# Two hybrid layers on one core: the convolution branch moved to the end, the sample states among the retention gates

## Chip, core and metric

The kernel runs on one core of a Trainium2 chip. The metric is the device time of one execution in microseconds: the median of 3 runs. TensorE (PE in the profile) multiplies, VectorE (DVE) and ScalarE (ACT) work on elements, GpSimd (POOL) does too and issues most of the small DMAs here, SyncE (SP) issues the weight loads.

## What is computed

Two layers on 256 prompt tokens and 8 sample tokens together, T = 264 columns, model width 1024. A layer (shortened from the reference):

```python
u = rmsnorm(h, norm_g);  z = u @ w_in
s5_out   = s5_branch(z[S5], h0, ...)        # complex diagonal state space, 32 groups x 64 states
ret_out  = retention_branch(z[Q], z[K], z[V], z[G], S0)   # 4 heads, key 128, value 256
conv_out = conv_branch(z[CONV], buf, ...)   # GLU, depthwise width 31, layer norm, silu
gates = sigmoid(z[GATE])
merged = gates[0] * (s5_out @ s5_proj) + gates[1] * (ret_out @ ret_proj) + gates[2] * (conv_out @ conv_proj)
h = h + merged @ w_out
h = h + (swiglu(rmsnorm(h)) if layer == 0 else moe_swiglu(rmsnorm(h)))   # top 2 of 8 experts

# state space:   h_t = lbar * h_(t-1) + Bbar u_t,   y = Re(C h) + D u, gelu, GLU
# retention:     inner = (q k^T * decay) v,   out = inner + (q S) * cross_decay
#                S' = gamma^c S + (k * k_decay)^T v;  group norm over the 256 values, times silu(g)
```

For a sample token the retention state of each head (128 x 256) is loaded, multiplied by gamma, gets the outer product of k and v, gives q S, and is stored: 8 samples x 4 heads, 512 KB a sample. The prompt starts from zero states. All arithmetic is fp32; the large products are made of three fp32r products of split operands.

## The kernel before, in words

Every engine has one program, written out by hand, and semaphores between them. Activations lie as [feature, token], so a tile of output is [128, 264], one PSUM bank. `tile_order()` lists all tiles in the order in which TensorE makes them; a tile's number modulo 8 is its bank, and a bank is opened when whoever evicts it has counted it. The same list orders the weights: `weight_tile` (L583) walks over blocks of 128x128, eight a chunk, in a ring of five chunks that SP fills. ScalarE makes the high part of each chunk (L976), VectorE the low part (L1283), both up to two chunks ahead of the tile that they are evicting. Three products of 264 columns a block (L577 to L579) give the tile. So where a helper of VectorE waits for something, the weights' low parts behind it wait too.

In a layer the order on TensorE is: convolution gate and value (cb, ca), state space input (zs), q, k, v; transposes (vt, vs, kt, ks: v and k as [token, feature], for prompt and samples), the state space matrices (win, kk), which GpSimd prepares; per head scores, output, state (sc, ou, st: L700 to L719), with one head's scores computed ahead; the state space drive of each 8-token chunk (si, L732); the convolution's layer norm sums (cm, cv, by ones, L610); then the sample loop, for b in 0..7: convolution gate gc(b) (8 blocks), the sample output os(b-1) (q times state, L749), convolution projection pc(b) (4 blocks), the outer products oa(b), ob(b) (L763); then the group norm sums (gm, gv, L610), the state space output y, the swish gates gg, yt, retention gate and projection gr, pr, the GLU gl, state space gate and projection gs, ps, the output wo, and the feed-forward part. Layer 0's is dense, layer 1's runs over experts.

VectorE does the 124 depthwise taps (31 by 4 blocks, L1377) in pieces: 16 beside zs, 32 beside v, 44 behind kt, 8 after each head's decay multiply (L1303). Then the 8 samples' convolution (L1303, L1460, L1462), the mean (L1468), the reciprocal (L1483). In the sample loop it steps the state space recurrence over 32 chunks of 8 tokens, 4 steps a sample, 5 small operations a step (tile rec), updates the sample's state (L1507) and masks k so that one row is left (L1475). ScalarE evicts, makes squares, roots (L1016), silus and high parts (L990).

GpSimd prepares the state space matrices (powers by doubling, L1746 to L1761), then issues: convolution states out (L1865, L1866), retention prompt state out (L1869), and per sample the store (L1873) and, when it has landed, the load of the sample after next (L1878) into one of two buffers. It prepares layer 1 after pr(7) of layer 0.

## Time and profile before

| | us |
|---|---|
| median of 3 runs | 2074.55 (2072.83 to 2078.42) |
| the profiled execution | 2078.8 |
| its span | 2076.7 |
| PE busy | 1953.4 (94%) |
| DVE busy | 1585.2 (76%) |
| ACT busy | 1171.4 (56%) |
| POOL busy | 348.5 (17%) |
| layer 1's experts, 1077 to 2067 | 990 |

Times in the rows are microseconds from the start of the span. "Busy" of PE is modelled for pipelined products. A stage's price is the stretch between two of its neighbours' starts on PE, and what stands in brackets behind a timeline row is how long the engine had been idle before it and who released it. A wait for several semaphores is put down to the last.

### The profile page before, as it was taken

What the parts mean: (1) busy time and instruction counts of PE and PEld (TensorE: products, weight loads), DVE (VectorE), ACT (ScalarE), POOL (GpSimd) and SP (SyncE); (2) the same over time, 40 slices, a digit from 0 to 9 for tenths busy, and PEclk for the clock granted to TensorE, in tenths of its full rate; (3) what the DMA queues carried; (4) which work ended last, traced back from release to release, by engine and by line L of the source; (5) the groups of instructions that cost most, each with busy time, mean ns of one, the idle gap of its engine ahead of it and who ended that gap; (6) DMA issues with size and microseconds to landing.
All of it is one profiled execution on the core that took longest, in us unless ns stands there. A gap on an engine that the chain in (4) does not pass through costs nothing.

```text
span 2076.7 us, 32156 instructions
## 1 busy us (share of the span) xinstructions
PE 1953.4 (94%) x12016; PEld 1657.9 (80%) x12016; DVE 1585.2 (76%) x1980; ACT 1171.4 (56%) x1209; POOL 348.5 (17%) x423
## 2 busy tenths in 40 slices
PE   7777999979998978999989999999999999999995
PEld 7766889979998977889977777777777777777774
DVE  6998855766545996746558888888888888888886
ACT  5333245444444443254456777767767776777775
POOL 7982100993000130100000000000000000000000
PEclk9989999989999997999969999999999999999998
DMA  5438625535555746535639999999999999999996
GB/s 195 143 91 137 219 75 167 184 110 183 183 173 154 213 101 137 157 112 181 242 141 355 368 383 351 387 360 365 371 370 378 354 379 364 370 371 366 382 358 233
DMA packets 98102, 527.57 MB, mean 254 GB/s; under 512 B 11864, under 2 KB 13432, under 8 KB 54360
## 3 DMA queue, kind: packets, MB, share of 16 engines
q1 hardware_dynamic: 86167, 488.69, 64.4%
q0 software_dynamic: 10784, 36.50, 8.2%
q8 instruction: 65, 1.06, 0.2%
q10 hardware_dynamic: 1056, 1.08, 0.1%
q14 instruction: 30, 0.24, 0.0%
HBM read 505.69 MB, written 20.54 MB: 253 GB/s over the span
## 4 chain that ended last, share of the span: by engine, by line
PE 78%; DVE 9%; POOL 6%; issue 3%; ACT 3%; DMA 1%; DVEq 0%; ACTq 0%; SPq 0%; POOLq 0%
PE bank L577 23%; PE bank L579 23%; PE bank L578 23%; POOL s5m L1761 3%; DVE zone L1377 3%; PE bank L763 1%; PE bank L749 1%; POOL work L1761 1%; DVE s5m_parts L1678 1%; PE bank L610 1%; PE bank L917 1%; PE bank L792 1%; PE bank L788 1%; ACT zone_parts L1229 1%; PE bank L872 1%
## 5 line engine op out<-in xcount | busy, mean ns | idle before, releaser
L1678 DVE TENSOR_TENSOR s5m_parts<-s5m,ring_parts 128x2048 fp32r<-128x2048 f32 x228 | 519.3, 2288 | 77.3 <-ACT ring_parts L1229 77.1
L1283 DVE TENSOR_TENSOR ring_parts<-ring,ring_parts 128x1024 fp32r<-128x1024 f32 x238 | 311.5, 1310 | 223.2 <-ACT ring_parts L976 221.9
L1229 ACT ACTIVATE ring_parts<-s5m 128x2048 fp32r<-128x2048 f32 x228 | 431.6, 1915 | 87.8 <-DMA s5m<-in_experts 81.7
L577 PE MATMUL bank<-uT_parts,ring_parts 128*128 128x264 f32 x1312 | 386.2, 294 | 39.4 <-DVE uT_parts L1300 21.0
L578 PE MATMUL bank<-uT_hi,ring_parts 128*128 128x264 f32 x1312 | 379.5, 289 | 0.0
L579 PE MATMUL bank<-uT_hi,ring_parts 128*128 128x264 f32 x1312 | 378.6, 289 | 0.0
L577 PE MATMUL bank<-s5m_parts,work_parts 128*112 128x512 f32 x896 | 359.1, 401 | 0.3 <-DVE table_parts L1671 0.3
L976 ACT ACTIVATE ring_parts<-ring 128x1024 fp32r<-128x1024 f32 x238 | 251.3, 1056 | 190.5 <-PE bank L579 169.0
L1678 DVE TENSOR_TENSOR s5m_parts<-s5m,zone_parts 128x2048 fp32r<-128x2048 f32 x112 | 255.9, 2288 | 67.1 <-ACT zone_parts L1229 66.9
L577 PEld LDWEIGHTS bank<-uT_parts,ring_parts 128*128 128x128 f32 x1312 | 254.4, 194 | 51.8 <-issue 45.5
L578 PEld LDWEIGHTS bank<-uT_hi,ring_parts 128*128 128x128 f32 x1312 | 255.3, 195 | 0.1
L579 PE MATMUL bank<-ring_parts,work_parts 128*112 128x512 f32 x640 | 254.1, 397 | 0.0
L579 PEld LDWEIGHTS bank<-uT_hi,ring_parts 128*128 128x128 f32 x1312 | 253.8, 193 | 0.0
L578 PE MATMUL bank<-ring_parts,table_parts 128*112 128x512 f32 x640 | 253.1, 396 | 0.0
L1229 ACT ACTIVATE zone_parts<-s5m 128x2048 fp32r<-128x2048 f32 x112 | 213.0, 1915 | 36.9 <-DMA s5m<-in_experts 35.3
L577 PEld LDWEIGHTS bank<-s5m_parts,work_parts 128*112 128x112 f32 x896 | 156.7, 175 | 49.5 <-issue 0.4
L577 PE MATMUL bank<-zone_parts,ring_parts 128*128 128x264 f32 x592 | 174.7, 295 | 8.8 <-DVE zone_parts L1300 8.8
L577 PE MATMUL bank<-s5m_parts,zone_parts 128*112 128x512 f32 x448 | 177.1, 395 | 0.0
L578 PEld LDWEIGHTS bank<-ring_parts,table_parts 128*112 128x112 f32 x640 | 113.0, 176 | 36.0
L579 PEld LDWEIGHTS bank<-ring_parts,work_parts 128*112 128x112 f32 x640 | 112.0, 175 | 37.1
L577 PEld LDWEIGHTS bank<-zone_parts,ring_parts 128*128 128x128 f32 x592 | 112.9, 191 | 10.4 <-issue 7.8
L1377 DVE SCALAR_TENSOR_TENSOR zone<-zone,vecs 128x256 f32<-128x256 f32 x240 | 117.1, 557 | 0.0
(283 smaller groups left out, 3126.5 us busy)
## 6 DMA issues: line engine op xcount, KB each, us to landing
s5m<-in_experts SPq DMA_DIRECT2D x340, 1024.0 KB, 6.7
ring<-in_weights SPq DMA_DIRECT2D x238, 512.0 KB, 3.3
work<-in_sret POOLq DMA_DIRECT2D x16, 512.0 KB, 4.7
out_ret_s<-work POOLq DMA_DIRECT2D x16, 512.0 KB, 4.8
s5m<-kscr POOLq DMA_DIRECT2D x16, 256.0 KB, 10.9
xT<-in_xT SPq DMA_DIRECT2D x1, 1056.0 KB, 5.1
zscr<-zone ACTq DMA_DIRECT2D x2, 528.0 KB, 5.8
work<-in_bc POOLq DMA_DIRECT2D x2, 512.0 KB, 4.9
```

The source lines that it names most:

```text
L577: pe.matmul(out, left[0], right[1], start=first, stop=False)
L578: pe.matmul(out, left[1], right[0], start=False, stop=False)
L579: return pe.matmul(out, left[0], right[0], start=False, stop=last)
L610: mm = pe.matmul(out[:, 0:T], ones[:, :], terms(i), start=(i == 0), stop=(i == n - 1))
L749: mm = pe.matmul(out[:, x:x + 1], sring[:, b % 2, h, half * P:(half + 1) * P], qs[:, h, b:b + 1], start=True, stop=True)
L763: mm = pe.matmul(out[:, x * DV:(x + 1) * DV], kmask[0:NS, b % 2, h * P:(h + 1) * P], vst[0:NS, h * DV:(h + 1) * DV], start=True, stop=True)
L976: act.activation(weights_hi(c), weights(c, ring), ACT.Copy).then_inc(high_done, 1)
L1229: act.activation(high_slot(c), slot(c, s5m), ACT.Copy).then_inc(high_done, 1)
L1283: dve.tensor_tensor(weights(c, ring_parts), weights(c, ring), f32(weights_hi(c)), ALU.subtract).then_inc(low_done, 1)
L1377: dve.scalar_tensor_tensor(out=cT[:, m, 0:SEQ], in0=xc[:, m, k:k + SEQ], scalar=vec(l, V_DWW, m * TAPS + k), in1=cT[:, m, 0:SEQ], op0=ALU. ...
L1678: dve.tensor_tensor(slot(c, s5m_parts), slot(c, s5m), f32(high_slot(c)), ALU.subtract).then_inc(low_done, 1)
L1761: last = pool.tensor_tensor(out[:, js], x[:, js], y[:, js], op)
```

## The change

It changes six things in each layer.

- The score product of the next head is no longer computed ahead: sc, ou, st for each head.
- The convolution's norm, gates and projections (cm, cv, gc, pc) move behind the state space projection: cm after ps(3), cv after ps(5), gc and pc after ps(7), before wo. The taps spread over more stages, by `CONV_AT` (how many a call, for layer 0 and layer 1). In layer 0, 0 beside zs, 8 beside v, 28 behind kt, 16 in the heads, 8 behind si, 48 beside pr, 16 in gs; in layer 1, 12, 24, 28, 12, 6, 32, 10.
- The sample loop stands beside the swish gates gg (8 blocks, no projection). The outer products take fp32r operands stacked on 72 rows (high, low, high part of v; high, high, low of k). The sample output is a product of q masked to one row, [128 x 8] by [128 x 256] for each head, all samples summed into one bank, copied and transposed once (ot). Banks: 7 rotate, the eighth takes long tiles. gr(0) stands before ot, gr(1) after y.
- The state space recurrence of 32 steps becomes a sweep. GpSimd makes the powers of the phase of lambda^8 (`turns`, by doubling, 5 complex products) and a damping tile; VectorE turns the drive back by them, scans it with real damping (two `tensor_tensor_scan` of 512 elements), and turns it forward again, at samples 2 to 6 of the loop.
- Four buffers for the sample states in place of two; sample b+4 is loaded into sample b's buffer.
- GpSimd issues the loads of samples 2 and 3 behind the convolution state's stores, makes the turns after si(3), and only then goes on to the stores. ScalarE masks k in VectorE's place. The preparation of layer 1 begins after the GLU.

```diff
+ROTATING = 7
+STACK = 72
+CONV_AT = {"zs": (0, 3), "v": (1, 3), "kt": (28, 28), "ret": (4, 3), "si": (8, 6), "gr": (6, 4), "gs": (6, 4)}
...
-        o += [((l, "sc", 0), 0)]
         for h in range(HEADS):
-            if h + 1 < HEADS:
-                o += [((l, "sc", h + 1), 0)]
-            o += [((l, "ou", h), 0), ((l, "st", h), 0)]
-        add("si", 4); add("cm", 1); add("cv", 1)
...
+            o += [((l, "sc", h), 0), ((l, "ou", h), 0), ((l, "st", h), 0)]
+        add("si", 4)
+        for b in range(NS):
+            o += [((l, "gg", b), KD)]
+            if b > 0:
+                o += [((l, "os", b - 1), 0)]
+            o += [((l, "oa", b), 0), ((l, "ob", b), 0)]
+        o += [((l, "os", NS - 1), 0), ((l, "gr", 0), KD), ((l, "ot", 0), 0)]
...
             o += [((l, "gs", d), KD), ((l, "ps", d), 4)]
+            if d == 3:
+                add("cm", 1)
+            if d == 5:
+                add("cv", 1)
+        for d in range(KD):
+            o += [((l, "gc", d), KD), ((l, "pc", d), 4)]
...
                     pe.wait_ge(*out_of((l, "ob", b)))
-                    for x in range(KD):
-                        h, half = x // 2, x % 2
-                        mm = pe.matmul(out[:, x:x + 1], sring[:, b % 2, h, half * P:(half + 1) * P],
-                                       qs[:, h, b:b + 1], start=True, stop=True)
+                    for h in range(HEADS):
+                        mm = pe.matmul(out[32 * h:32 * h + NS, 0:DV], qm[:, h, b * NS:(b + 1) * NS], states[b % 4][:, h, :],
+                                       start=False, stop=(b == NS - 1))
...
-                            mm = pe.matmul(out[:, x * DV:(x + 1) * DV], kmask[0:NS, b % 2, h * P:(h + 1) * P],
-                                           vst[0:NS, h * DV:(h + 1) * DV], start=True, stop=True)
+                            mm = pe.matmul(out[:, x * DV:(x + 1) * DV], kmask_parts[0:STACK, b % 2, h * P:(h + 1) * P],
+                                           vst_parts[0:STACK, h * DV:(h + 1) * DV], start=True, stop=True)
...
+                    act.activation(kmask_parts[0:STACK, b % 2, :], f32(kst_parts[0:STACK, :]), ACT.Copy,
+                                   scale=pick[0:STACK, b:b + 1]).then_inc(kmask_ready, 1)
...
+            def sweep(l, d):
...
+                if d == 2:
+                    dve.wait_ge(turns_ready, l + 1)
...
+                    mul(driven, si[:, :, :, 0:NC], both).then_inc(dve_order, 1)
+                    mul(swept[:, 0], si[:, 1, :, 0:NC], im).then_inc(dve_order, 1)
...
+                elif d == 3:
+                    link(add(driven[:, 0], driven[:, 0], swept[:, 0]))
+                    link(dve.tensor_tensor(driven[:, 1], driven[:, 1], swept[:, 1], ALU.subtract))
+                    link(dve.tensor_tensor_scan(swept[:, 0].rearrange("p j t -> p (j t)"), damp,
+                                                driven[:, 0].rearrange("p j t -> p (j t)"), 0.0, ALU.mult, ALU.add))
...
+                for d in range(KD):
+                    merge("gs", "ps", 0, d)
+                    if d < 3:
+                        conv_ops(l, "gs")
+                    if d == 2:
...
+                        sampled_conv()
+                    if d == 4:
+                        conv_mean()
+                    if d == 5:
+                        conv_norm()
...
+                pool.wait_ge(mm_done, DONE[(l, "si", 3)])
...
+                n = 1
+                while n < NC:
+                    product([turns[:, r, :, n:2 * n] for r in range(2)], [turns[:, r, :, 0:n] for r in range(2)],
+                            [turns[:, r, :, n - 1:n].broadcast_to([P, GJ, n]) for r in range(2)], cross[:, :, 0:n])
+                    n *= 2
...
-                    if b + 2 < NS:
+                    if b + 4 < NS:
 
                         pool.wait_ge(mm_done, DONE[(l, "os", b)])
-                        pool.wait_ge(s_out[b % 2], 16 * (4 * l + b // 2 + 1))
+                        pool.wait_ge(s_out[b % 4], 16 * (2 * l + b // 4 + 1))
```

GpSimd's program of layer 0, from the matrices' way through memory to the first samples. Before:

```order
L1859 DMA s5m<-kscr 16x32x128 x8
L1865 DMA out_conv_p<-zone 512x1x30
L1866 DMA out_conv_s<-zone 4096x1x30
L1869 DMA out_ret_p<-zone 128x4x256
L1873 DMA out_ret_s<-work 128x4x256
L1878 DMA work<-in_sret 128x4x256
L1873 DMA out_ret_s<-work 128x4x256
L1878 DMA work<-in_sret 128x4x256
```

After, with the turns between the prompt state's store and the first sample's:

```order
L1995 DMA zone<-in_sret 128x4x256 x2
L1996 DMA out_ret_p<-zone 128x4x256
L2001 COPY s5m<-lw 128x16 x2
L2002 COPY s5m<-lw 128x512
L2003 MEMSET s5m 128x16
L1872 TENSOR_TENSOR s5m<-s5m 128x16 x2
L1878 TENSOR_TENSOR s5m<-s5m 128x16
L1872 TENSOR_TENSOR s5m<-s5m 128x16 x2
L1881 TENSOR_TENSOR s5m<-s5m 128x16
L1872 TENSOR_TENSOR s5m<-s5m 128x16x2 x2
L1878 TENSOR_TENSOR s5m<-s5m 128x16x2
```

Twelve more rows of such products follow (to 128x16x16) before `L2013 DMA out_ret_s<-work 128x4x256`, which came right behind the prompt state's store.

VectorE in layer 0, the samples' convolution and the layer norm. Before, ahead of the sample loop (cT lies in zone):

```order
L1303 TENSOR_TENSOR tmp<-zone,vecs 128x248
L1460 TENSOR_REDUCE zone<-tmp 128x8
L1462 TENSOR_SCALAR zone<-zone,vecs 128x8
L1303 TENSOR_TENSOR tmp<-zone,vecs 128x248
L1460 TENSOR_REDUCE zone<-tmp 128x8
L1464 TENSOR_SCALAR zone<-zone,vecs 128x8
L1468 SCALAR_TENSOR_TENSOR zone<-bank,zone 128x1056
L1475 TENSOR_SCALAR work<-work,ident 8x512 x2
L1483 RECIPROCAL rstd<-bank 128x264
L1303 TENSOR_TENSOR zone<-zone,rstd 128x1056
L1300 TENSOR_TENSOR zone_parts<-zone,sq_parts 128x264 x4
```

After, it stands in the state space gates gs, between merges (tmp<-bank,gate is gate times projection), with the weights' low parts:

```order
L1344 TENSOR_TENSOR ring_parts<-ring,ring_parts 128x1024 x2
L1364 TENSOR_TENSOR tmp<-bank,gate 128x264
L1367 TENSOR_TENSOR zone<-zone,tmp 128x264
L1640 SCALAR_TENSOR_TENSOR zone<-bank,zone 128x1056
L1344 TENSOR_TENSOR ring_parts<-ring,ring_parts 128x1024
L1364 TENSOR_TENSOR tmp<-bank,gate 128x264
L1367 TENSOR_TENSOR zone<-zone,tmp 128x264
L1647 RECIPROCAL rstd<-bank 128x264
L1364 TENSOR_TENSOR zone<-zone,rstd 128x1056
L1344 TENSOR_TENSOR ring_parts<-ring,ring_parts 128x1024 x2
L1364 TENSOR_TENSOR tmp<-bank,gate 128x264
L1367 TENSOR_TENSOR zone<-zone,tmp 128x264
```

The same two operations of the norm (the mean, now L1640, and the reciprocal, now L1647) have five low parts and three merges between and behind them.

VectorE in the sample loop of layer 0, one sample. Before, with its four recurrence steps (tile rec):

```order
L1283 TENSOR_TENSOR ring_parts<-ring,ring_parts 128x1024 x2
L1303 TENSOR_TENSOR zone<-bank,gate 128x264
L1507 SCALAR_TENSOR_TENSOR work<-work,bank 128x256 x4
L1475 TENSOR_SCALAR work<-work,ident 8x512
L1303 TENSOR_TENSOR rec<-s5m,l 128x32
L1303 TENSOR_TENSOR rec<-s5m,l 128x16 x2
L1306 TENSOR_TENSOR rec<-rec,work 128x32
L1306 TENSOR_TENSOR s5m<-rec 128x32
L1303 TENSOR_TENSOR rec<-s5m,l 128x32
```

After, samples 2 and 3 with the sweep's first pieces:

```order
L1344 TENSOR_TENSOR ring_parts<-ring,ring_parts 128x1024
L1586 SCALAR_TENSOR_TENSOR work<-work,bank 128x256 x4
L1364 TENSOR_TENSOR s5m<-work,s5m 128x1024
L1364 TENSOR_TENSOR s5m<-work,s5m 128x512 x2
L1344 TENSOR_TENSOR ring_parts<-ring,ring_parts 128x1024
L1586 SCALAR_TENSOR_TENSOR zone<-zone,bank 128x256 x4
L1367 TENSOR_TENSOR s5m<-s5m 128x512
L1486 TENSOR_TENSOR s5m<-s5m 128x512
L1487 SCALAR_TENSOR_TENSOR s5m<-s5m 128x512
L1344 TENSOR_TENSOR ring_parts<-ring,ring_parts 128x1024
```

The small operations are gone; a sample has a wide piece of the sweep in their place.

## Rows read from the trace of the kernel before

**Rows 1.** The chain that ended last, pieces in order of time: start us, us, what
```profile
176.74 2.06 PE bank L610 x8
...
185.34 1.82 DVE rstd L1483
...
211.79 1.92 PE bank L763 x8
...
259.75 3.56 PE bank L610 x8
...
868.05 7.56 PE bank L610 x20
```

**Rows 2.** Windows: window, us, busy us (x instructions) of PE, PEld, DVE, ACT, POOL, PEclk, DMA share, GB/s
```profile
172.00:191.00 19.00, 11.79 (x154) 10.16 (x149) 9.48 (x19) 8.60 (x14) 0.79 (x1) 0.91 1.07 98
191.00:260.00 69.00, 66.62 (x457) 60.99 (x458) 57.84 (x231) 18.85 (x32) 11.65 (x16) 0.95 0.68 208
...
1077.00:2067.00 990.00, 973.08 (x4368) 735.45 (x4367) 837.95 (x544) 713.15 (x488) 27.03 (x32) 0.99 0.96 361
```

**Rows 3.** Timeline of PE: start us, us, engine line op out<-in [idle before <-releaser]
```profile
152.09 0.70 PE L700 MATMUL bank<-zone 128*128 128x256 f32 x2
...
161.81 0.60 PE L712 MATMUL bank<-work,zone 128*128 128x256 f32 x2
...
163.99 0.59 PE L700 MATMUL bank<-zone 128*128 128x256 f32 x2
...
171.34 3.94 PE L732 MATMUL bank<-s5m 128*64 128x48 f32 x128
...
191.50 0.56 PE L577 MATMUL bank<-zone_parts,ring_parts 128*128 128x264 f32 x1 [3.78 <-DVE zone_parts L1300]
...
748.84 0.70 PE L700 MATMUL bank<-zone 128*128 128x256 f32 x2
...
756.93 1.19 PE L712 MATMUL bank<-work,zone 128*128 128x256 f32 x2 [6.52 <-DVE work L1303]
```

**Rows 4.** Timeline of ACT, 379 to 384 us
```profile
379.10 0.39 ACT L1164 ACTIVATE gate<-bank 128x264 f32<-128x264 f32 x1 [1.77 <-PE bank L579]
...
383.48 0.39 ACT L1164 ACTIVATE gate<-bank 128x264 f32<-128x264 f32 x1 [0.34 <-PE bank L579]
```

**Rows 5.** Timeline of POOL, 239 to 246 and 365 to 390 us
```profile
239.92 0.75 POOL L1873 DMA_DIRECT2D out_ret_s<-work  x1 [1.34 <-DVE work L1507]
245.44 0.76 POOL L1878 DMA_DIRECT2D work<-in_sret  x1 [4.76 <-PE bank L579]
...
365.09 0.73 POOL L1746 TENSOR_TENSOR work<-work 128x16 f32<-128x16 f32 x2
...
374.60 4.07 POOL L1807 COPY work<-work 128x32 f32<-128x32 f32 x8
...
379.71 1.31 POOL L1746 TENSOR_TENSOR work<-lw,work 128x256 f32<-128x256 f32 x2
...
386.00 3.11 POOL L1761 TENSOR_TENSOR s5m<-work 128x256 f32<-128x256 f32 x3
```

**Rows 6.** DMA issues of 160 to 230 us: KB each, median us to landing
```profile
work<-in_sret POOLq DMA_DIRECT2D x5, 512.0 KB, 4.6
...
out_ret_s<-work POOLq DMA_DIRECT2D x4, 512.0 KB, 5.1
...
out_conv_s<-zone POOLq DMA_DIRECT2D x1, 480.0 KB, 27.6
```

**Rows 7.** Groups on DVE, 205 to 253 us: out<-in xcount | busy, mean ns | idle before
```profile
L1283 DVE TENSOR_TENSOR ring_parts<-ring,ring_parts 128x1024 fp32r<-128x1024 f32 x9 | 11.0, 1226 | 1.8 <-ACT ring_parts L976 1.6
L1507 DVE SCALAR_TENSOR_TENSOR work<-work,bank 128x256 f32<-128x256 f32 x24 | 8.9, 416 | 1.4 <-PE bank L763 1.2
```

**Rows 8.** Groups on DVE, 376 to 403 us, beside POOL's preparation
```profile
L1283 DVE TENSOR_TENSOR ring_parts<-ring,ring_parts 128x1024 fp32r<-128x1024 f32 x9 | 13.7, 1520 | 4.6 <-ACT ring_parts L976 4.6
```

**Rows 9.** Timeline of DVE, the first operation of the sampled convolution
```profile
171.94 0.40 DVE L1303 TENSOR_TENSOR tmp<-zone,vecs 128x248 f32<-128x248 f32 x1
```

More of the change, by code:

```diff
@@ L135, in tile_counts @@
     place, done, chunk = {}, {}, []
-    n = b = 0
+    n = b = turn = long = 0
     for i, (key, blocks) in enumerate(tile_order()):
-        place[key] = i
+        if key[1] == "os" or i > 0 and key[1] in ("ms1", "ms2"):
+            place[key] = long * NBANK + ROTATING
+            long += key[1] != "os" or key[2] == NS - 1
+        else:
+            place[key] = turn // ROTATING * NBANK + turn % ROTATING
+            turn += 1
         if key[1] in ("ms1", "ms2") and i > 0:
@@ new lines, in _, with gate_of @@
+                masked(0)
+                masked(1)
+                for b in range(NS):
+                    key = (l, "gg", b)
+                    full(key)
+                    act.activation(mT[:, b, :], at(key)[:, 0:T], ACT.Silu).then_inc(freed(key), 1)
+                    if b + 2 < NS:
+                        masked(b + 2)
+                def gate_of(name, d, of):
+                    key = (l, name, d)
+                    full(key)
+                    act.activation(gate[:, of, :], at(key)[:, 0:T], ACT.Sigmoid).then_inc(freed(key), 1)
@@ new lines, in _ @@
+                key = (l, "os", NS - 1)
+                copy_out(key, os_rows, at(key)[:, 0:DV])
+                gate_of("gr", 0, 0)
+                key = (l, "ot", 0)
+                full(key)
+                for half in range(2):
+                    last = act.activation(vT[:, half:KD:2, SEQ:T],
+                                          at(key)[:, half * P:(half + 1) * P].rearrange("p (h x) -> p h x", h=HEADS)[:, :, 0:NS],
+                                          ACT.Copy)
+                last.then_inc(freed(key), 1)
@@ new lines, in _, with merge @@
+                for d in range(KD):
+                    key = (l, "pr", d)
+                    evicted_by_act((l, "gr", d))
+                    full(key)
+                    dve.wait_ge(gated, KD * (l + 1))
+                    mul(mT[:, d, :], at(key)[:, 0:T], gate[:, d % 2, :]).then_inc(freed(key), 1)
+                    if d == 4:
+                        for m in range(4):
+                            low((l, "y", m), yg[:, m, :])
+                    conv_ops(l, "gr")
+                def merge(gate_name, proj_name, turn, d):
+                    key = (l, proj_name, d)
+                    evicted_by_act((l, gate_name, d))
+                    full(key)
+                    mul(tmp[:, d % 2, :], at(key)[:, 0:T], gate[:, d % 2, :]).then_inc(freed(key), 1)
+                    evicted_by_act(key)
+                    if turn == 0:
+                        evicted_by_act((l, "pr", d))
+                    else:
+                        dve.wait_ge(merged, 16 * l + d + 1)
+                    add(mT[:, d, :], mT[:, d, :], tmp[:, d % 2, :]).then_inc(merged, 1)
```

452 lines of the change are left out of this document (252 added, 200 removed).

## The prediction, made before the result was known

> **What bounds the kernel now.** The profiled execution took 2078.8 us, with a span of 2076.7, against a median of 2074.55 (2072.83 to 2078.42). I sum against the execution's own time and take 4.25 off at the end.
>
> I read first the chain that ended last, for the places where it leaves TensorE, then the stretches in a table of windows, then TensorE's, ScalarE's and GpSimd's timelines there. The expert half, 990 us of layer 1, has TensorE at 98% and is not edited [rows 2]. The edited part of layer 0 runs from its first score product at 152.09 [rows 3] to the first group-norm sum at 259.75 [rows 1], 107.7 us. In layer 1 it is 748.84 [rows 3] to 868.05 [rows 1], 119.2 us. See in it three losses: ahead of layer 1's first output product TensorE waits 6.52 us for the decay multiply that stands behind 44 convolution taps on VectorE (in layer 0 2.7 less, by the same reading); in 172 to 191 it is busy 11.8 of 19 us, since the chain goes through the layer norm, sum, square, root, reciprocal of 1.82, silu [rows 1, 2]; and it then waits 3.78 for the first half of the convolution output [rows 3]. The sample loop, 191 to 260, has TensorE at 66.6 of 69 us [rows 2]: it is bound by products, not by VectorE's recurrence.
>
> **The change part by part.** I recompute the stretch from first score to first group-norm sum.
>
> Heads and s-inputs. Before, 152.09 to 175.28 in layer 0, where the 128 small products end (171.34 + 3.94), 23.2 us [rows 3]. Now no score is computed ahead, so a head is its output products and its state, 2.18 (161.81 to 163.99), its scores, 0.8 (to 164.8), and the decay multiply, which lay beside the state before and is now bare: two products of 256 and 128 columns, 0.8 estimated from VectorE's 0.42 for 256 [rows 3, 7]. Sum 3.75, up to 5 if the handovers are counted in full. Only 28 taps stand before it instead of 44, so that wait goes. ScalarE's three extra small copies put 1.5 ahead. 1.5 + 4 x 3.75 + 3.9 = 20.4 in layer 0. Layer 1 lost 2.7 more [rows 3], 26 before; I allow it 1 more for the taps that still stand in the heads, so 21.4.
>
> Convolution norm. The stretch 175.3 to 191.5, 16.2 us, is gone from here in layer 0, and about as much in layer 1.
>
> Sample loop. Before, 68.3 (191.5 to 259.75) and some 77 to the end. A sample was a gate tile of 8 blocks, a projection of 4, four outer products at 1.92 [rows 1] and 0.5 for the output vector. Twelve blocks take 4.38 (379.10 to 383.48 [rows 4]), so 8 take 2.92: the total was about 8.2. Now the gate tile of 2.92, outer products that are single-pass on stacked halves but with 72 rows, and four output products. No row shows either. From below, a single-pass product of 264 columns takes 4.38 / 36 = 0.12, four 0.49; from above, the 1.92 that four fp32 ones of 256 columns take. I take 0.49 for the outer products, since their operands are of the single-pass kind now, and 1.92 for the output, whose operands are fp32: 5.3. PE alone would need 43 for eight.
>
> But VectorE stands still at sample 2 until the turns are there, and GpSimd forms them only after the convolution state's issues and the last s-input product. Price: five doubling products of six operations. GpSimd does the like in its preparation: three products on 16, 32 and 64 elements a partition from 365.09 to 374.60, 9.5 us, and one on 256 from 379.71 to 386.00, 6.3 [rows 5]. The turns are the sizes 16 to 64 (9.5), 128 (4.5, between these) and 256 (6.3 at most, 5 with VectorE idle), and two small copies, a wide one and a memset, 1.9, estimated from 0.51 a copy [rows 5]: 21 to 22.5 us. Then the state traffic: a store issues, lands after 5.1, and only then the load into its buffer issues, landing after 4.6 [rows 6]. The queue is in order, so each of the four reloads costs GpSimd the store's landing and its own issue, 5.1 + 0.76 = 5.9 us, or 6.3 by the issues at 239.92 and 245.44 [rows 5]; I take 5.9. The last lands at 22.5 + 23.6 + 4.6 = 51 us after the loop's start, then VectorE's update of four at 0.42 [rows 7] the handovers to and from it, and the output products, 58 us in layer 0, 60 in layer 1, where the convolution state's 480 KB, landing after 27.6 [rows 6], and the heads lie closer together. With the first residual gate (2.92) and the transposes with their copies (1.2) it is 62.1 and 64.1.
>
> Together 82.5 against 107.7 and 85.5 against 119.2, plus what comes back later: two sums of four products, 3.9; eight convolution projections, 8 x 1.46 = 11.7; less the gate tile already done, 2.9: 12.7. Gain here: 12.5 and 21.0.
>
> The recurrence becomes a sweep. 160 small operations a layer (most of VectorE's 231 instructions in the loop, which keep it busy 57.8 of 69 us [rows 2]) are replaced by 15 wide ones, 1.2 for the 1024-element ones [rows 7] and 0.6 to 1 for 512, some 11 us. It hides behind TensorE before and now; it costs nothing and gives nothing, except with the waits above. The scan is not in this trace; its bounds are 0.6 (a 512-element tensor operation) and 2.4, and both are covered.
>
> State space projection stage (gs and ps), where the convolution now ends. Here the taps, the sampled convolution and the layer norm now lie beside TensorE's 4.38 a step. Before, VectorE had two weight halves (1.23) and two multiplies (0.43), 3.3 of 4.38 [rows 4, 7]. With 6 taps of 0.4 it needs 5.7 for three steps, and the sampled convolution adds 4.8 (171.94 [rows 9] to 176.7, where the mean's sum starts [rows 1]): the mean's sum after the fourth step waits 5.3 in layer 0 and, with 4 taps a step, 1.7 in layer 1. The square, root, reciprocal (1.82 [rows 1]) and four silus form one chain that crosses three times between ScalarE and VectorE among the weight halves. Its legs before were 4 to 5 us (188 to 191.5 the last), against the 4.38 of a step: one step is overrun by 3.6, an estimate, in each layer. The first convolution projection waits 0.5 for its low half, the stage's start 0.5. GpSimd prepares layer 1 there and slows the halves from 1.23 to 1.52 [rows 7, 8], which over some ten halves that are now on the path is 3.5 in layer 0 alone. Sum 13.4 and 6.3.
>
> The rule of this contention in the Trainium skill ("SBUF — State Buffer", 🔬 SBUF: two separate sides): a VectorE operation with two SBUF inputs and a GpSimd operation that reads SBUF hold one port pair as a lock, and the loser stands. The trace agrees in direction: 1226 ns alone, 1520 beside GpSimd's products [rows 7, 8]. By it GpSimd would be the loser as often as VectorE, and the same 24% on 22.5 us of turns brings them 5 us later: the second rival.
>
> Other terms: the first residual gate stands at hand when the group norm's outcome is waited for, taken as -0.5 a layer; GpSimd's two memsets before the end of layer 0's preparation, which VectorE waits for, -1, and four small copies fewer ahead of it, at 0.4 to 0.5 each [rows 5], +1.6. The start's twenty small VectorE operations lie under the preparation of layer 0 (nothing). Sum: 12.5 + 21.0 - 13.4 - 6.3 - 1 - 1 + 1.6 = 13.4, from 2078.8 to 2065.4 for the profiled execution, and 2061 as median.
>
> **Rivals.**
> - The turns and the reloads don't decide. For it: the outer products and outputs sum to 43 us only if nothing stands; VectorE's buffers allow two samples ahead; before, GpSimd's issues waited for VectorE and TensorE, not for a transfer (1.34 and 4.76 idle [rows 5]). Against: the turns' small operations cost their issue, not their size: 9.5 us for three products of 16 to 64 elements [rows 5]. If GpSimd is done in 12 us, the loop takes 45: 13 less in each layer, with the norm chain half hidden: near 2035. Chance 0.27.
> - No change to speak of, 2074. GpSimd and VectorE hold each other up: turns 5 us later in each layer (the 24% above), and each of four reloads at 6.3 in place of 5.9: loop 65 and 66, 13 more than forecast in all. For it: the 6.3 us of the widest product were measured beside VectorE's halves, and these suffered too [rows 8]. Against: VectorE itself waits at sample 2 and then leaves GpSimd alone. Chance 0.17.
> - Slower. The layer norm among the gates serialises. For it: 172 to 191 shows how long its chain is, 19 us, when nothing else stands on VectorE [rows 2]. In the new place each leg stands behind halves that TensorE needs itself. ScalarE and VectorE prepare two chunks ahead, 5.8 us of TensorE's work; each of four legs (sampled convolution, mean, norm, silu with its high halves) that returns later than that stops TensorE. If all do, the chain's 19 us and the 4.8 of the sampled convolution are bare in each layer, 24 instead of 13.4 and 6.3: 2078.8 - 33.5 + 48 + 0.4 = 2093.7, less 4.25 = 2089. It decides from 5.8 us a leg. Chance 0.11.
> - That the scores without the head start cost more than 3.75 a head is inside the forecast's own range: a head at 5 gives +5 a layer.
>
> **How the numbers follow.** Forecast 2061 with chance 0.45; its own range is 2051 to 2072 (loop +-4, norm stage +-4 in each layer, the start +-2). The first rival is 2028 to 2046, the second 2067 to 2080, the third above 2081. The range 2034 to 2081 leaves about half of the first rival's chance and most of the third's outside. A difference of 0.3%, 6.2 us, is what can be told: faster is below 2068.3. That is all of the first rival (0.27), four fifths of the forecast (0.38) and a part of the second (0.03): 0.68. Slower is above 2080.8: 0.11. The rest, 0.21, is the same.
>
> **What would show it.** In the changed profile: a wait of VectorE for GpSimd's s5m tile at the third sample, about 8 to 12 us; reload issues some 5.9 us apart; a loop of 58 to 60 us with TensorE busy for 43; a wait of TensorE before the mean's sum of 5 and 2 us and before the norm's of about 4; layer 1's expert half unchanged at 990. Wrong it would be if VectorE doesn't wait there, if the outer products take 1.9 again, or if more than 15 us stand in either norm stage.

## The result, and the profile after

The changed kernel takes 2086.6 us (median of 11 runs, 2080.1 to 2091.5) against 2074.0 of the kernel before on the same chips; the ratio is 1.0056 (95% interval 1.0042 to 1.0069). It is 12 us slower. The forecast was 2061, the range 2034 to 2081. The profiled execution took 2091.5 us with a span of 2089.7; it was the slowest of the eleven, 4.9 above the median, and that of the kernel before lies 4.8 above its own.

A stage is the stretch from one first product on TensorE to the next. The numbers are differences between starts of such products in the two timelines; the kernel before's first two are in [rows 1, 3].

| stage, layer 0 / layer 1 | before | after | difference | forecast |
|---|---|---|---|---|
| start to the first score | 152.1 | 148.5 | -3.6 | about -0.6 |
| first score to group-norm sum | 107.7 / 119.2 | 89.5 / 88.2 | -18.1 / -31.0 | -25.2 / -33.7 |
| group-norm sum to transposes yt | 50.8 / 52.0 | 40.1 / 40.8 | -10.6 / -11.2 | -19.9 / -19.9 |
| yt to the feed-forward norm | 99.7 / 96.0 | 150.6 / 142.7 | +50.8 / +46.7 | +46.5 / +39.4 |
| feed-forward norm to layer 1's first score | 338.6 | 330.5 | -8.1 | 0 |
| layer 1's feed-forward norm to the end | 1060.6 | 1058.7 | -1.9 | 0 |

The forecast column is the prediction's terms: eight swish gates (23.4 us) leave the third stage, one gate tile (2.9) enters it and 0.5 is taken as lost there; 33.1 us of products and 13.4 or 6.3 of waits enter the fourth. The differences sum to +13.0, the spans' difference; the forecast's sum to -13.4. The windows of the changed kernel's stages (window, us, busy us and instructions of PE, PEld, DVE, ACT, POOL, clock, DMA share, GB/s):

```profile
171.20:238.10 66.90, 43.39 (x318) 37.13 (x317) 33.76 (x62) 21.33 (x32) 25.02 (x49) 0.85 0.80 205
238.10:278.20 40.10, 31.77 (x248) 22.21 (x249) 18.06 (x26) 12.85 (x25) 0.00 (x0) 0.91 0.04 14
278.20:428.80 150.60, 136.31 (x1058) 132.40 (x1058) 124.67 (x189) 72.93 (x116) 95.39 (x115) 0.97 0.47 151
...
785.30:847.50 62.20, 47.37 (x348) 40.43 (x345) 33.87 (x62) 21.23 (x32) 24.83 (x49) 0.79 0.78 207
847.50:888.30 40.80, 32.48 (x249) 22.48 (x249) 18.06 (x26) 12.87 (x25) 0.00 (x0) 0.87 0.04 14
888.30:1031.00 142.70, 136.06 (x1058) 133.92 (x1058) 100.27 (x167) 72.90 (x116) 1.95 (x3) 0.95 0.47 155
1088.00:2078.00 990.00, 975.09 (x4376) 737.06 (x4375) 839.16 (x547) 713.72 (x489) 22.82 (x32) 0.99 0.95 360
```

Read them against [rows 2]. The sample loop of 171 to 238 has TensorE at 43 of 67 us where it was 66.6 of 69: the products got fewer, but the stretch did not. In 238 to 278, where a loss of only 0.5 us was forecast, TensorE is busy 32 of 40, VectorE 18 and ScalarE 13. None of them is full, so they wait for each other or for a DMA, and the DMA share is only 0.04. (The window that begins at 785.30 takes in the last s-input products of layer 1; its loop begins at 786.83 and takes 60.6 us.) Layer 1's experts are unchanged at 990.

**The group norm.** TensorE's timeline (start, us, operation, idle time before it and who ended it), then VectorE's and ScalarE's of the same stretch:

```profile
254.32 0.63 PE L816 MATMUL bank<-s5m 64*40 64x128 f32 x8
259.04 1.05 PE L812 MATMUL bank<-s5m 128*40 128x128 f32 x4 [4.09 <-DVE rstd L1609]
...
269.07 0.95 PE L812 MATMUL bank<-s5m 128*40 128x128 f32 x4 [3.99 <-DVE rstd L1609]
```

```profile
249.17 0.78 DVE L1364 TENSOR_TENSOR zone<-zone 128x264 f32<-128x264 f32 x2
256.40 0.78 DVE L1361 TENSOR_TENSOR zone_parts<-zone,work_parts 128x264 fp32r<-128x264 f32 x2 [6.45 <-ACT work_parts L1022]
257.09 1.80 DVE L1609 RECIPROCAL rstd<-bank 128x264 f32<-128x264 f32 x1
```

```profile
250.48 1.07 ACT L1026 ACTIVATE s5m<-bank 40x512 f32<-40x512 f32 x2 [4.04 <-PE bank L816]
254.98 1.07 ACT L1026 ACTIVATE s5m<-bank 40x512 f32<-40x512 f32 x2 [3.43 <-PE bank L816]
255.95 0.73 ACT L1022 ACTIVATE work_parts<-zone 128x264 fp32r<-128x264 f32 x2
```

The products L812 and L816 are the state space output y. ScalarE makes the high half of a row (L1022), and VectorE subtracts it from the row to get the low half (L1361). After four y tiles TensorE waits 4.1 us for the bank that VectorE's third reciprocal (L1609) frees. That reciprocal starts at 257.09, behind the low halves of the first two gated rows (L1361), for which VectorE stood 6.45 us: they need ScalarE's high halves (L1022, 255.95), and in ScalarE's program these stand behind the evictions of four y tiles (L1026, the second pair at 254.98), which TensorE had to make first. The same turn comes round at 269.07, and both again in layer 1. A reciprocal takes 1.8 us in both kernels, so the operations did not get slower.

**The sample loop.** GpSimd's timeline, from the last turn operation on (L2013 a store, L2018 a reload), VectorE's at sample 2, and TensorE's products:

```profile
188.65 0.19 POOL L2009 COPY s5m<-s5m 128x1 f32<-128x1 f32 x1
189.18 0.79 POOL L2013 DMA_DIRECT2D out_ret_s<-work  x1 [0.34 <-issue]
202.34 0.77 POOL L2018 DMA_DIRECT2D work<-in_sret  x1 [12.37 <-DMA out_ret_s<-work]
...
210.60 0.76 POOL L2018 DMA_DIRECT2D work<-in_sret  x1 [6.74 <-PE bank L782]
...
216.62 0.75 POOL L2018 DMA_DIRECT2D zone<-in_sret  x1 [4.52 <-DMA out_ret_s<-zone]
...
224.31 0.75 POOL L2018 DMA_DIRECT2D zone<-in_sret  x1 [6.19 <-PE bank L767]
```

```profile
188.87 2.43 DVE L1364 TENSOR_TENSOR s5m<-work,s5m 128x1024 f32<-128x1024 f32 x3 [3.30 <-POOL s5m L2009]
194.84 1.23 DVE L1344 TENSOR_TENSOR ring_parts<-ring,ring_parts 128x1024 fp32r<-128x1024 f32 x1 [3.54 <-issue]
...
198.76 1.23 DVE L1487 TENSOR_TENSOR_SCAN s5m<-s5m 128x512 f32<-128x512 f32 x1
```

```profile
183.07 0.62 PE L767 MATMUL bank<-work,qm 128*8 128x256 f32 x8
183.62 0.74 PE L782 MATMUL bank<-work_parts 72*128 72x256 f32 x4
...
197.54 1.04 PE L767 MATMUL bank<-zone,qm 128*8 128x256 f32 x8 [6.14 <-DVE zone L1586]
...
232.17 1.04 PE L767 MATMUL bank<-zone,qm 128*8 128x256 f32 x8 [7.35 <-DVE zone L1586]
```

The turns are ready at 188.8, 17.5 us after they began: that term was too large (21 to 22.5). But the first store, issued at 189.18, is seen to land only at 202.3, 12.4 us of idle time where 5.1 was taken [rows 6], because 480 KB of convolution state in 120-byte rows, issued at 163, lie ahead of it (experiments 2 and 4 test this). Where the row of a reload names a product of TensorE, here and below, that product was already done; what the reload waited for last is the landing of the store from the same buffer. The outer products take 0.74 us, against 1.92 in [rows 1], and the four output products 0.62, so that TensorE alone needs 4.1 us a sample, 33 in all, not 43. VectorE at sample 2 waited for the turns (L2009), but only 3.3 us where 8 to 12 were forecast. After its first piece of the sweep it stood another 3.5 us (the row at 194.84): its next wait is for the state of sample 2, whose load was issued at 168.4 and took some 26 us to land. So at sample 2 of layer 0 not the turns were last but the load behind the same clogged queue; in layer 1 VectorE waited 5.8 us for the turns and none for the load. The waits of TensorE that follow in layer 0 are 6.1, 2.0, 4.0 and, at the last sample, 7.4 us.

**The layer norm among the gates.** TensorE stands before the mean's sum (L635 waits for the mean's operand, L1634) and once more before a weight's low half (L1344). TensorE's rows in layer 0, then its waits in layer 1 from 850 on (line waited for, total us, times, longest):

```profile
352.36 1.25 PE L635 MATMUL bank<-zone,ones 128*128 128x264 f32 x2 [6.06 <-DVE zone L1634]
...
378.21 0.40 PE L602 MATMUL bank<-uT_parts,ring_parts 128*128 128x264 f32 x1 [4.22 <-DVE ring_parts L1344]
```

```profile
PE bank L812 <- DVE rstd L1609: 8.1, 2, 4.1
PE bank L602 <- DVE ring_parts L1344: 3.6, 1, 3.6
PE bank L635 <- DVE zone L1634: 3.0, 1, 3.0
```

### The profile page after: what moved, and what is told of

The parts are those of the page before. It is cut to its first block, busy times and chain, and to the rows that moved or that the text cites. A ratio compares the mean times of both kernels' runs of the same rounds, so it can differ in the third digit from the quotient of the medians.

```text
span 2089.7 us, 31546 instructions
## 1 busy us (share of the span) xinstructions
PE 1915.8 (92%) x11832; PEld 1619.3 (77%) x11832; DVE 1536.9 (74%) x1702; ACT 1187.0 (57%) x1225; POOL 364.2 (17%) x489
## 4 chain that ended last, share of the span: by engine, by line
PE 73%; DVE 7%; POOL 7%; issue 4%; DMA 4%; ACT 4%; DVEq 0%; ACTq 0%; POOLq 0%; SPq 0%
PE bank L602 22%; PE bank L604 22%; PE bank L603 22%; POOL s5m L1887 3%; DVE zone L1468 2%; DMA out_ret_s<-work 1%; DVE s5m_parts L1804 1%; POOL work L1887 1%; DMA out_ret_s<-zone 1%; PE bank L812 1%; PE bank L816 1%; PE bank L949 1%; PE bank L635 1%; POOL s5m L1872 1%; ACT zone_parts L1290 1%
## 5 line engine op out<-in xcount | busy, mean ns | idle before, releaser
L1344 DVE TENSOR_TENSOR ring_parts<-ring,ring_parts 128x1024 fp32r<-128x1024 f32 x238 | 309.7, 1305 | 235.9 <-ACT ring_parts L1008 207.3
L1302 ACT ACTIVATE s5m<-bank 112x512 f32<-112x512 f32 x56 | 33.5, 597 | 141.4 <-PE bank L604 141.4
```

The costliest lines, as they stand in the source:

```text
L1302: act.activation(hm[0:CAP, t % 2, :], bank[t % 2][0:CAP, :], ACT.Silu).then_inc(evicted[t % 2], 1)
L1344: dve.tensor_tensor(weights(c, ring_parts), weights(c, ring), f32(weights_hi(c)), ALU.subtract).then_inc(low_done, 1)
```

## The experiments

Every run is compared with the kernel before on its own chip; gains against another experiment are differences of medians, good to some 4 us. By the ratios the same gains come out up to 3 us larger or smaller; where that matters it is said.

**1. The ring.** The low halves of the gated rows go behind all reciprocals.

```diff
-                    if h > 0:
-                        for m in (2 * h - 2, 2 * h - 1):
-                            low((l, "r", m), vT[:, m, :])
-                for m in (KD - 2, KD - 1):
+                for m in range(KD):
                     low((l, "r", m), vT[:, m, :])
```

> Base: the changed kernel, 2086.6. The low halves of the normed retention rows stand behind all four reciprocals here, not between them. Theory A (ring of waits in the group norm: the fifth y tile waits for a bank that a reciprocal frees, the reciprocal stands behind low halves that wait for ScalarE's high halves, and these stand behind evictions of y tiles): the two waits of TensorE of 4 us ahead of y products go, with the slow clock behind them, 8 to 10 us in each layer, so 2067 to 2071. Theory B (the reciprocals of 1.8 and their multiplies are themselves too slow, order is no matter): within 3 us of 2086.6. Theory C (gone there, but the retention projection then waits for the late low halves): 2078 to 2083.

Measured: 2067.25, ratio 0.9950 (0.9933 to 0.9966), 19 us less than the changed kernel. VectorE's timeline in it:

```profile
248.58 0.78 DVE L1364 TENSOR_TENSOR zone<-zone 128x264 f32<-128x264 f32 x2
249.28 1.80 DVE L1609 RECIPROCAL rstd<-bank 128x264 f32<-128x264 f32 x1
...
252.55 1.80 DVE L1609 RECIPROCAL rstd<-bank 128x264 f32<-128x264 f32 x1
...
255.82 0.77 DVE L1361 TENSOR_TENSOR zone_parts<-zone,work_parts 128x264 fp32r<-128x264 f32 x2
```

The reciprocals follow each other at 3.3 us, nothing waits between, and the stage takes 28.9 us in both layers, down from 40.1 and 40.8. Theory A holds, with 11 and 12 us of stage in the two layers. The edit leaves the seven banks as they are, so what the eighth bank would have given is not tested.

**2. The convolution state's store.** It is issued behind the last sample's store.

```diff
-                pool.dma_start(a["conv_s"][l], xs[:, :, :, 1:TAPS]).then_inc(conv_state_out, 16)
...
+                pool.dma_start(a["conv_s"][l], xs[:, :, :, 1:TAPS]).then_inc(conv_state_out, 16)
                 pool.wait_ge(h_ready, l + 1)
```

> Base 2086.6. The store of the samples' convolution state (480 KB in 120 B rows) is issued behind the last sample's store, not ahead of the loads of samples 2 and 3. Theory A (that store clogs the queue: sample 2's load lands late and the first sample's store needs 12.4 us, so all reloads are late): the first store lands in 5 to 6 us, the loop loses 6 to 10 us of stall in each layer, 2068 to 2075. Theory B (the turns and the serial store and reload set the loop): 2083 to 2087. Theory C (the store then collides with the weight loads later): above 2087.

Measured: 2076.9, ratio 1.0011 (0.9992 to 1.0030), 10 us less than the changed kernel: nearest to theory A, a little short of its range. Its executions spread widely (2068.1 to 2090.6). The profiled one, among the fastest, has the loop at 58.2 and 57.8 us in place of 66.9 and 60.6, and its first store lands after 3.9 us of waiting, not 12.4.

**3. Both.**

> Both edits. If the two costs are independent, the gains add: 2050 to 2059. If they share one slack (TensorE ends both stretches on the same chain), not more than the larger alone, 2067 to 2071.

Measured: 2055.5, ratio 0.9899 (0.9883 to 0.9915). 19 and 10 less than 2086.6 are 2057: they add. These two edits alone turn 0.56% slower into 1.0% faster.

**4 and 5. What the turns cost, with the store in the way and without.** Four of the five turn products are left out, `while n < NC` becoming `while n < 2`, in the changed kernel and in experiment 3; the state space states are then wrong, so these two only price the turns.

> Base 2086.6. Leaves out four of the five doubling products of the turns (the state space states are then wrong); GpSimd is done with them some 14 us earlier. Theory A (the convolution state's store sets when the first sample's store lands, at 202): the loop is shorter by 0 to 3 us in each layer, 2081 to 2086. Theory B (the prediction's: turns, then four serial reloads of 5.9): 10 to 14 us in each layer, 2058 to 2066.

> Base: the kernel with both edits, e3_both, 2055.5. Leaves out four of the five turn products (state space states wrong). Theory A (with the convolution state's store out of the way the turns of 17.5 us are what holds VectorE at sample 2, and the reloads after it): 6 to 12 us less, 2043 to 2050. Theory B (the queue and the serial stores and reloads set the loop even so): within 3 us of 2055.5.

Measured: 2089.8, ratio 1.0063 (1.0045 to 1.0082), no gain; and 2040.8, ratio 0.9832 (0.9812 to 0.9852), 15 us less than experiment 3 and more than theory A's 12. GpSimd in the two, first 4, then 5:

```profile
176.09 0.19 POOL L2009 COPY s5m<-s5m 128x1 f32<-128x1 f32 x1
181.25 0.79 POOL L2013 DMA_DIRECT2D out_ret_s<-work  x1 [4.98 <-DVE work L1586]
201.73 0.77 POOL L2018 DMA_DIRECT2D work<-in_sret  x1 [19.69 <-DMA out_ret_s<-work]
```

```profile
180.52 0.79 POOL L2009 DMA_DIRECT2D out_ret_s<-work  x1 [3.16 <-DVE work L1586]
188.61 0.77 POOL L2014 DMA_DIRECT2D work<-in_sret  x1 [7.31 <-PE bank L767]
```

In 4 the first store leaves 8 us earlier and still lands at 201.7, 19.7 us of waiting: the queue decides, and the turns are free behind it. In 5, with the queue clear, the turns count: without them the loop takes 54.8 and 49.9 us, from 61.4 and 58.2. The prediction had the right place, and the chain was real, but it was the second in line.

**6. The scores one head ahead again**, on experiment 3 (`sc(h + 1)` opened and multiplied before `ou(h)`, as before).

> Base e3_both, 2055.5. The next head's scores are computed one head ahead again, as in the kernel before. The bare decay multiply costs 0.8 us a head for three heads of two layers, 4.9 us. Theory A (that wait is on the path): 2049 to 2053. Theory B (VectorE and GpSimd's later milestones, the loop's turns and reloads, absorb it, since they start by the states and s-inputs anyway): 2054 to 2056.

Measured: 2045.15, ratio 0.9866 (0.9841 to 0.9891), 10 us less than experiment 3 (7 by the ratios, whose intervals overlap), where at most 6 were expected. The heads and the s-inputs take 17.3 and 17.5 us in place of 23.0 and 29.7 in the profiled executions; 5.8 of layer 1's are a stop of TensorE that comes and goes (below). The loop keeps its length (60.8 and 59.5 us for 61.4 and 58.2), so the heads' time is on the path in full.

**7. The taps out of the state space gates**, on experiment 3.

```diff
-CONV_AT = {"zs": (0, 3), "v": (1, 3), "kt": (28, 28), "ret": (4, 3), "si": (8, 6), "gr": (6, 4), "gs": (6, 4)}
+CONV_AT = {"zs": (0, 3), "v": (1, 3), "kt": (28, 28), "ret": (4, 3), "si": (8, 6), "gr": (8, 6), "gs": (0, 0)}
```

> Base e3_both, 2055.5. The 16 and 10 taps that stand among the state space gates go to the retention gates (8 and 6 a step there). Theory A (the mean's sum waits 6.0 and 3.0 us for these taps): 9 less, minus what 8 taps a step cost among the retention gates, 2047 to 2051. Theory B (the sampled convolution of 4.8 us and the chain behind it set the wait, or the taps overrun the retention gates' step of 5.84): 2053 to 2060.

Measured: 2053.8, ratio 0.9892 (0.9869 to 0.9915), the same as experiment 3. The mean's sum waits 4.9 and 2.4 us in place of 6.0 and 3.0: theory B, the taps are not what it waits for.

**8. Store ahead of the reload**, on experiment 3: the store of sample b + 1 is issued before GpSimd waits for sample b's.

```diff
-                    if b + 4 < NS:
...
-                        pool.wait_ge(mm_done, DONE[(l, "os", b)])
...
+                    if 1 <= b < 5:
+                        c = b - 1
+                        pool.wait_ge(mm_done, DONE[(l, "os", c)])
...
```

> Base e3_both, 2055.5. GpSimd issues the store of sample b+1 before it waits for the store of sample b and issues its reload. Theory A (the serial store, landing and reload sets samples 6 and 7, each reload 6 to 8 us apart): the two last waits of 4 and 5 us shrink, 3 to 6 us in each layer, 2044 to 2050. Theory B (the reload waits for TensorE's output product or VectorE's update, which themselves wait for the turns): within 3 us of 2055.5, or later by as much.

Measured: 2041.9, ratio 0.9846 (0.9823 to 0.9870), 14 us less (11 by the ratios), at or just beyond the upper end of theory A's 6 to 12. GpSimd in experiment 3, then in 8:

```profile
189.54 0.79 POOL L2009 DMA_DIRECT2D out_ret_s<-work  x1 [0.34 <-issue]
193.60 0.77 POOL L2014 DMA_DIRECT2D work<-in_sret  x1 [3.27 <-DMA out_ret_s<-work]
194.37 0.75 POOL L2009 DMA_DIRECT2D out_ret_s<-work  x1
201.62 0.75 POOL L2014 DMA_DIRECT2D work<-in_sret  x1 [6.50 <-PE bank L604]
```

```profile
189.34 1.55 POOL L2009 DMA_DIRECT2D out_ret_s<-work  x2 [0.34 <-issue]
193.36 0.75 POOL L2014 DMA_DIRECT2D work<-in_sret  x1 [2.48 <-DMA out_ret_s<-work]
194.59 0.75 POOL L2009 DMA_DIRECT2D out_ret_s<-zone  x1 [0.48 <-issue]
196.62 0.76 POOL L2014 DMA_DIRECT2D work<-in_sret  x1 [1.28 <-PE bank L782]
```

The second reload issues at 196.6 and not at 201.6, and the loop takes 49 and 52 us, from 61 and 58. So once the queue is clear, the serial chain of stores and reloads that the prediction named counts, beside the turns.

**9. The late convolution store alone in the kernel before.**

> Base: the kernel before, 2074 to 2077. Only the store of the samples' convolution state moves behind the sample loop. Theory A (the clog costs only where four buffers and turns put GpSimd's first store behind it; before, the loop is bound by TensorE at 66.6 of 69 us): within 4 us. Theory B (the queue that it fills also holds up weights and states in the kernel before): 5 to 10 us faster.

Measured: 2076.5, ratio 1.0002 (0.9989 to 1.0016). That is theory A: there the same clog is free, with TensorE busy 66.6 of the loop's 69 us [rows 2].

**10. The recurrence back in place of turns and sweep**, on experiment 3: GpSimd's turns and `sweep` go out, `recur(l, 4 * d, 4 * d + 4)` and the l8 copies come back.

> Base e3_both, 2055.5. The sweep and the turns are taken out and the recurrence of 32 steps stands in the sample loop again, 4 steps a sample. Theory A (the sweep costs a wait of 17.5 us for GpSimd; VectorE with the recurrence needs 3.2 + 1.23 + 1.66 = 6.1 us a sample, 49 in all, less than the loop's 59): 5 to 10 us a layer faster, 2036 to 2046. Theory B (the prediction's: it gives and costs nothing, the reloads set the loop): 2053 to 2058. Theory C (VectorE becomes the bound at 7.5 us and more a sample): above 2058.

Measured: 2048.8, ratio 0.9871 (0.9851 to 0.9890), 7 us less, at the edge of the noise, and between theories A and B. The profiled loop is clearly shorter, 54.5 and 53.7 us. The sweep relieves VectorE, which had no need of it here, and charges GpSimd 17.5 us ahead of its first store.

**11. All together, with the recurrence.**

> Low halves behind the reciprocals, convolution store late, scores one head ahead, recurrence in place of turns and sweep, stores and reloads pipelined. If the gains add (e6_scores_ahead -10, e10_recurrence -7 against e3_both, some of e8): 2036 to 2041. If the recurrence makes VectorE the bound of the loop so that the rest is hidden: 2044 to 2049.

Measured: 2043.8, ratio 0.9858 (0.9836 to 0.9880). It doesn't add, and lies just below the second theory's range. The loop is 55.1 and 53.5 us, as in experiment 10, so the pipelined reloads gave it nothing; VectorE is busy 47 of it, against 34 in experiment 8, whose loop with the sweep and the same reloads is 49.5 and 52.4. That VectorE now sets it is the reading that fits. So the sweep is worth its price only after both faults of the queue are mended.

**12. The outer products in fp32 on 8 rows again**, on experiment 3.

> Base e3_both, 2055.5. The outer products are fp32 on 8 rows again, 1.92 us in place of 0.74 for the four. Theory A (the loop waits for GpSimd's turns and reloads, so TensorE has room): 0 to 7 us slower, 2055 to 2062. Theory B (TensorE's time in the loop counts in full): 8 x 1.2 in each layer, 19 us slower, 2074.

Measured: 2060.6, ratio 0.9932 (0.9910 to 0.9953), 5 us slower (7 by the ratios), at the edge of the noise and far from 19: the loop hides most of them, theory A.

**13 and 14. The layer norm's place**, on experiment 8. In 13 the root stands ahead of the eviction of gate gs(6) on ScalarE; in 14 the taps are as in 7 and the samples' convolution follows the first merge, not the third.

```diff
+                    if d == 6:
+                        root((l, "cv", 0), 1.0 / 512)
                     gate_of("gs", d, d % 2)
...
                     if d == 6:
-                        root((l, "cv", 0), 1.0 / 512)
```

> Base e8_reload_pipelined, 2041.9. ScalarE's root for the layer norm stands ahead of the seventh state space gate's eviction, not behind it. Theory A (VectorE stands at the reciprocal with the weights' low halves behind it until TensorE has made the seventh gate tile, and TensorE then waits 4.2 and 3.6 for low halves): these waits shrink to below 1, 5 to 8 us faster, 2034 to 2037. Theory B (the length of the chain sum, root, reciprocal, silu, high halves sets it, wherever the root stands): within 3 us, with the wait elsewhere.

> Base e8_reload_pipelined, 2041.9. All taps end in the retention gates and the samples' convolution stands behind the first state space merge, not the third. Theory A (the mean's sum waits 6 and 3 us since the samples' convolution, 4.8 us, stands two steps too late): the waits go, 6 to 9 us with the slow clock behind them, 2033 to 2036. Theory B (VectorE is full there: what is moved ahead is missed at the first steps): 2040 to 2044.

Measured: 2038.05, ratio 0.9826 (0.9807 to 0.9844), and 2038.6, ratio 0.9821 (0.9800 to 0.9842): 4 and 3 us less (4 and 5 by the ratios), between the theories, and each by itself inside the noise. The profiled stage of yt to the feed-forward norm shows them more sharply: 153.4 and 141.3 in experiment 8, 147.7 and 140.0 in 13, 147.9 and 137.4 in 14. Of the 9.4 us of 14, 5.7 are lost again in layer 0's loop (55.2 us for 49.5), which was not looked into. In 13 the wait for low halves is gone in layer 0 and is 2.2 us, from 3.6, in layer 1. In 14 the wait for the mean's sum is gone and what stays in layer 1 is the wait for low halves:

```profile
PE bank L602 <- DVE ring_parts L1344: 4.4, 2, 3.6
```

**15. The best**: 8, 6, 13 and 14 together, sweep kept.

> Both of these and the scores one head ahead, with the sweep kept. Adds up to 2041.9 - 10 - 6 - 6 = 2020 if each is on the path by itself; if the heads' gain is taken up by the loop's turns, and the two of the norm share one chain, 2030 to 2035.

Measured: 2024.0 (2022.9 to 2031.8), ratio 0.9773 (0.9748 to 0.9798), 49 us under the kernel before by the medians and 47 by the ratio, with nothing left out. It lies between "all adds" (2020) and the shared path (2030 to 2035), nearer to the first. The stages: heads and s-inputs 17.7 and 23.3 (the second with a stop of TensorE, below), loop 49.4 and 51.1, group norm 28.9 and 28.9, yt to the feed-forward norm 144.3 and 136.3.

## Why the prediction was wrong

- **The failed step is the group norm's.** "The first residual gate stands at hand when the group norm's outcome is waited for, taken as -0.5 a layer": the stage between the loop and yt was passed over as a moved gate tile. The diff shows the multiplies by the swish gate and the low halves between the reciprocals, the high halves between ScalarE's y evictions, and seven rotating banks where there were eight. Each reads as harmless; the order of the low and high halves closes a ring through three engines. It cost 9.3 and 8.7 us against the forecast of the stage, 18 of the 26.4 us by which the sum of the profiled stages missed. Experiment 1 gives back 19.
- **The loop: right mechanism, wrong first in line.** 58 and 60 us to the last output product and 62.1 and 64.1 to the group norm were forecast, from the turns, then four reloads at 5.9. The turns took 17.5, less than taken. The store of 480 KB was known to need 27.6 us [rows 6] and was used only for 2 us more in layer 1, not for the first store, which waited 12.4 behind it, nor for sample 2's load. Reload issues came 8.3, 6.0 and 7.7 apart. The loop took 66.9 us in layer 0, 4.8 too much, and 60.6 in layer 1, 3.5 less than forecast. Layer 1's loss lies in the heads and s-inputs ahead of it, 27.6 for 21.4, of which 5.3 are a stop of TensorE (below); in layer 0 they took 22.6 for 20.4. First score to group norm came out at 89.5 and 88.2 for 82.5 and 85.5: +7.0 and +2.7. Experiments 2, 4, 5 and 8 show the order: queue, then turns and reloads.
- **TensorE's own time in the loop** was forecast too high (5.3 a sample, measured 4.1), since the output products were put at 1.92 and took 0.62. It did not matter, as TensorE did not set the loop; experiment 12 shows that even 1.2 us more a sample count for little more than a third.
- **A reading of the kernel before:** layer 1's loop, put at "some 77" us, is 72.9 from its first convolution projection at 795.16 to 868.05, and the stretch ahead of it 20.4, not "about as much" as 16.2. The forecast starts from the two together, so nothing in its sum hangs on it.
- **The recurrence** "costs nothing and gives nothing": as a term it held, with the waits priced apart. Experiment 10 puts the exchange at some 7 us with the queue clear, and 11 shows the sign turn round when reloads are pipelined.
- **The layer norm.** 13.4 and 6.3 forecast, 17.7 and 13.6 measured (150.6 and 142.7 less 99.7 and 96.0 and 33.1 of added products); in layer 0 that is beyond the 15 us named as a sign of being wrong. The waits were right: TensorE's idle time in the stage grew by 13.0 and 6.6 us, with 6.1 and 3.0 before the mean's sum for a forecast 5.3 and 1.7, and 4.2 and 3.6 before low halves for 3.6 each. What was missed is its busy time, 4.9 and 6.9 us more than the added products: the granted clock of the stage is 0.97 and 0.95, in the kernel before 0.98 and 1.00.
- **The feed-forward part.** Nothing was forecast, and 8.1 us came back in layer 0. GpSimd's preparation of layer 1 starts at 330 in place of 362 and is over when the feed-forward products begin. In the 61 us behind the norm GpSimd had been busy 46.6, with TensorE at 57.5 and a granted clock of 0.88; now GpSimd is idle there and TensorE at 61.0 and 0.96. This is read from the two traces, not tested.
- **The rivals.** The lock of the shared port (the second: turns 5 us later, loops of 65 and 66) was hardly put to the test: the turns came earlier than the estimate, and VectorE was busy only 5.3 of their 17.7 us. The third rival, a full serial chain of 24 us a layer and 2089, has a total near what came, but by luck: the norm's stage cost 17.7 and 13.6, and its missing part is close to what the group norm cost.
- The start gained 3.6 us where 0.6 was taken; the cause was not tested.

What stays open: how much of TensorE's longer busy time in the layer norm's stage is the slower clock alone; what the seventh and eighth bank do to the ring; and 13, 14 and the heads together gave 18 us over experiment 8, where 13 and 14 were not run together without the heads.

## What to carry to other kernels

Where a change interleaves two engines' lists, follow the new order as a ring: for each wait ask what stands ahead of the producer on its own engine, then on the next, and with rotating buffers include who frees the buffer; cheap moves can close a circle that no busy time shows (TensorE, VectorE and ScalarE none of them full, DMA idle). A big store in small rows belongs behind the transfers that someone waits for, and where one engine issues stores and loads in turn, a wait for a landing belongs behind the next issue. Relieving one engine is worth little while the engine that takes the work over is late with its first transfer for it.

## What the runs showed of the hardware

The four output products, [128 x 8] by [128 x 256] in fp32, each writing 8 rows at another quarter of the bank, take 0.62 us together, where four fp32 outer products of 256 columns on 8 rows took 1.92 [rows 1]. That the four overlap because their outputs stand 32 rows apart is the reading that fits; it is not tested.

The scan of 512 elements (L1487 above) took 1.23 us, the plain operation of 512 elements just ahead of it (L1486) 0.69. That is the rate that the Trainium skill ("DVE: opcode table, instruction layouts, handler registers and perf-mode slots", 6. Datapath and trigger behaviour) gives for the built-in scan, half throughput; the trace agrees.

TensorE stops in the middle of the s-inputs of layer 1 or of the first gate tile of layer 0 with no releaser. The product after the stop, and the DMA queues of 776 to 788 us (packets, MB, share of 16 engines):

```profile
784.96 1.95 PE L751 MATMUL bank<-s5m 128*64 128x48 f32 x32 [5.28 <-issue]
```

```profile
q0 software_dynamic: 529, 1.71, 109.9%
q8 instruction: 1, 0.02, 0.9%
```

In that stretch the packets of the software queue alone take 109.9% of the 16 engines' time, and one packet of instructions passes. The stop in the s-inputs is 5.3 us here and in experiment 1, 5.8 in 3, 6.7 in 8, 5.6 in 13, 3.0 in 15 and absent in the other profiles of changed kernels; the one in layer 0's first gate tile is in all of them, 2.3 to 3.5 us (3.1 here, at 176.82), and the kernel before has one of 2.6 at 779.76. That TensorE's own program is late behind the state loads is the reading that fits; it was not tested. One profile a kernel can't tell whether these stops make up the spread of some 10 us between executions.
